# Hybrid block: input normalised before its hi/lo split, gates evicted by ScalarE, ten columns a turn

## What is computed

```python
h = rmsnorm(x, norm_g); proj = h @ w_in
v, bg, cg, za, u, zb, ga, gb = split(proj)      # u, zb: 1024 wide; the others 2048
ya = (bg * causal_conv3(cg * v, conv_w) * silu(za)) @ w_out_a
yb = gelu(s5_scan(u, ...))                       # 64 groups of 64 complex states
yb = yb * sigmoid(yb @ w_glu + b_glu)
yb = (yb * silu(zb)) @ w_out_b
m = sigmoid(ga) * ya + sigmoid(gb) * yb
x = rmsnorm(x + m @ w_o, final_g)
```

## Time and profile before

| | |
|---|---|
| median of 3 runs | 2556.7 us (2553.48 to 2559.24) |
| span of the profiled execution | 2557.4 us; no time of its own is given beside its span |
| TensorE busy | 2394.3 us, 94% of the span, 20536 matmuls |
| VectorE busy | 1687.3 us, 66% |
| ScalarE busy | 967.6 us, 38% |
| GpSimd busy | 331.2 us, 13%, nearly all of it before 626 us |
| DMA | 388.57 MB, mean 152 GB/s |
| mean granted TensorE clock | 0.946 |

### The profile page before, as it was taken

How to read it: one execution, slowest core, us unless ns; L and a number is a source line. 1 busy time by engine, 2 the same in 40 slices (tenths; PEclk the granted TensorE clock), 3 DMA queues, 4 the chain that set the end, 5 groups by cost and what they waited for, 6 DMA issues and landing times.

```text
span 2557.4 us, 52642 instructions
## 1 busy us (share of the span) xinstructions
PE 2394.3 (94%) x20536; PEld 2292.1 (90%) x20536; DVE 1687.3 (66%) x2202; ACT 967.6 (38%) x1164; POOL 331.2 (13%) x200
## 2 busy tenths in 40 slices
PE   7988888889999999789998799899999999999997
PEld 7988888888999999789997577669999999999997
DVE  8688888887555598856698644457656656654444
ACT  4433333333544434343443312234443434433442
POOL 0255555554000000200001100000000000000000
PEclk9999999999999999999998677889999999999999
DMA  6543334433555555345554000015555555556554
GB/s 222 190 141 138 139 139 139 139 138 133 197 191 186 181 172 197 131 156 187 188 169 154 20 2 2 18 60 187 183 188 188 181 188 187 182 170 189 188 181 135
DMA packets 107132, 388.57 MB, mean 152 GB/s; under 512 B 11952, under 2 KB 12080, under 8 KB 106800
## 3 DMA queue, kind: packets, MB, share of 16 engines
q1 hardware_dynamic: 103968, 374.39, 43.2%
q0 software_dynamic: 2080, 8.91, 1.0%
q10 hardware_dynamic: 1008, 4.17, 0.4%
HBM read 385.32 MB, written 2.10 MB: 151 GB/s over the span
## 4 chain that ended last, share of the span: by engine, by line
PE 75%; DVE 13%; issue 7%; POOL 3%; ACT 1%; DVEq 0%; DMA 0%; POOLq 0%; ACTq 0%
PE ps_main L1420 22%; PE ps_main L1421 22%; PE ps_main L1422 22%; DVE w_lo L774 3%; POOL turns L380 2%; PE ps_main L1607 1%; PE ps_aux L1607 1%; PE ps_main L1730 1%; PE ps_main L1731 1%; POOL h_state L384 1%; PE ps_aux L1697 1%; PE ps_aux L1696 1%; DVE f_val L940 1%; DVE m L901 1%; PE ps_main L1613 1%
## 5 line engine op out<-in xcount | busy, mean ns | idle before, releaser
L774 DVE TENSOR_TENSOR w_lo<-w_raw,w_hi 128x1024 fp32r<-128x1024 f32 x718 | 935.1, 1315 | 491.2 <-ACT w_hi L460 477.3
L460 ACT ACTIVATE w_hi<-w_raw 128x1024 fp32r<-128x1024 f32 x718 | 747.0, 1046 | 823.3 <-PE ps_main L1422 814.9
L1420 PE MATMUL ps_main<-xh,w_hi 128*128 128x256 f32 x1792 | 524.4, 293 | 45.3 <-DVE w_lo L774 33.5
L1421 PE MATMUL ps_main<-xl,w_hi 128*128 128x256 f32 x1792 | 513.8, 287 | 0.0
L1422 PE MATMUL ps_main<-xh,w_lo 128*128 128x256 f32 x1792 | 512.6, 286 | 0.0
L1420 PEld LDWEIGHTS ps_main<-xh,w_hi 128*128 128x128 f32 x1792 | 350.4, 196 | 60.6 <-DVE w_lo L774 37.0
L1420 PE MATMUL ps_main<-x3h,w_hi 128*128 128x256 f32 x1408 | 394.4, 280 | 0.0
L1421 PE MATMUL ps_main<-x3l,w_hi 128*128 128x256 f32 x1408 | 392.8, 279 | 0.0
L1422 PE MATMUL ps_main<-x3h,w_lo 128*128 128x256 f32 x1408 | 392.8, 279 | 0.0
L1421 PEld LDWEIGHTS ps_main<-xl,w_hi 128*128 128x128 f32 x1792 | 350.5, 196 | 0.5
L1422 PEld LDWEIGHTS ps_main<-xh,w_lo 128*128 128x128 f32 x1792 | 349.8, 195 | 0.0
(11 more groups left out here) (369 smaller groups left out, 3926.8 us busy)
## 6 DMA issues: line engine op xcount, KB each, us to landing
w_raw<-wmain SPq DMA_DIRECT2D x622, 512.0 KB, 3.3
w_raw<-wdown SPq DMA_DIRECT2D x80, 512.0 KB, 3.6
b_stage<-bst POOLq DMA_DIRECT2D x8, 512.0 KB, 5.4
w_raw<-wdown SPq DMA_DIRECT2D x16, 256.0 KB, 2.7
bias<-bias POOLq DMA_DIRECT2D x8, 384.0 KB, 3.3
x_res<-xt ACTq DMA_DIRECT2D x4, 512.0 KB, 10.8
out<-x_res SPq DMA_DIRECT2D x4, 512.0 KB, 2.6
c_raw<-cs ACTq DMA_DIRECT2D x1, 1024.0 KB, 16.7
```

Of the source, the lines that this page charges most:

```text
L460: nc.scalar.activation(whi[:, s, 0:width], raw[:, s, 0:width], ACT.Copy).then_inc(hi_ready, 1)
L774: V.tensor_tensor(wlo[:, s, 0:width], raw[:, s, 0:width], whi[:, s, 0:width].bitcast(F32), ALU.subtract)\
L1420: nc.tensor.matmul(out, whi[:, s, w], xh_[:, k, :], start=(first and kk == 0), stop=False)
L1421: nc.tensor.matmul(out, whi[:, s, w], xl_[:, k, :], start=False, stop=False)
```

## The change

- The input comes first: x is loaded through two queues, ahead of the weights; ScalarE squares it, VectorE adds in pieces, TensorE sums over the partitions, GpSimd multiplies x by norm_g, VectorE by `rstd`, ScalarE rounds and VectorE takes the rest, in five pieces (`PIECES`), which the first column's matmuls follow. No result needs `rstd` any more. As u and silu(zb) now lie where x lay, x is loaded again during `outb`.
- Gates, u and v are read from PSUM by ScalarE (`drain`); the ways through `tz` and the multiplications by `rstd` go.
- ga moves into the turns: ten columns (za, v, cg, bg, ga, twice), ga in a bank of `aux`, copied out by ScalarE, its sigmoid taken later in `gb`. `gaa` becomes `outa`, 16 columns. The scan's steps get new places.
- c_prime goes to GpSimd. The gelu result is split during `outa`, its rounding on ScalarE; so is the rounding of f in `outb`.
- hi and lo of a tensor are one tensor; counts are renumbered.

```diff
-STREAM = [("u", 8, 2), ("zb", 8, 2), ("conv", 64, 2), ("gb", 16, 2), ("gaa", 32, 2), ("glu", 8, 1),
+STREAM = [("u", 8, 16), ("zb", 8, 16), ("conv", 64, 160), ("gb", 16, 32), ("outa", 16, 32), ("glu", 8, 8),
...
-        SCAN_BU, SCAN_IN, SCAN_Y = (0, 0, 3, 3), (0, 1, 3, 4), (3, 4, 6, 7)
+        SCAN_BU, SCAN_IN, SCAN_Y = (0, 0, 3, 3), (0, 1, 4, 5), (4, 5, 8, 9)
+        KINDS = ("za", "v", "cg", "bg", "ga") * 2
+        PIECES = ((0, 2), (2, 4), (4, 8), (8, 12), (12, 16))
...
         def _(sp):
+            for c in (0, 2):
+                sp.dma_start(x[:, 4 * c:4 * c + 4, :], x_dram[:, 4 * c:4 * c + 4, :]).then_inc(x_loaded[c], 16)
             for s in range(RING):
                 sp.dma_start(raw[:, s, :], wmain[s]).then_inc(w_loaded[s], 16)
+            sp.dma_start(const[:, :], const_dram).then_inc(const_loaded, 16)
...
+            for k in range(4):
+                pool.wait_ge(xsq_ready, k + 1)
+                nc.gpsimd.tensor_tensor(x[:, 4 * k:4 * k + 4, :], x[:, 4 * k:4 * k + 4, :],
+                                        par[:, c + 4 * k:c + 4 * k + 4].unsqueeze(2).to_broadcast([P, 4, L]),
+                                        ALU.mult).then_inc(xg_ready, 1)
...
+            pool.wait_ge(yo_ready, SB)
+            for c in range(4):
+                pool.dma_start(x[:, 4 * c:4 * c + 4, :], x_dram[:, 4 * c:4 * c + 4, :]).then_inc(x_again, 16)
...
+            def conv(i, i0, last=False):
+                for p, kind in enumerate(KINDS):
+                    split_hi(n + 3)
+                    split_hi(n + 4)
+                    if p == 9 and not last:
+                        trig(i + 1)
+                    if kind == "za":
+                        finished(n + 1)
+                        act.wait_ge(ya_ready, At(2 * i0 + q + 1, 2, i).v())
+                        drain(ACT.Silu, gt[:, q, :], bank(g), g)
+                    elif kind == "v":
+                        finished(n + 1)
+                        drain(ACT.Copy, vbuf, bank(g), g)
+                    elif kind == "ga":
+                        finished(n + 1)
+                        nc.scalar.activation(slot(sga, j) ..., aux[:, 3, 0:L], ACT.Copy).then_inc(ga_copied, 1)
...
             n0 = UNIT0["outb"]
-            with act.Fori(0, 4) as i:
-                for b in range(4):
-                    split_hi(At(n0 + b + 3, 4, i))
+            for b in range(16):
+                split_hi(At(n0 + b + 3))
+                act.wait_ge(f_ready, b + 1)
+                nc.scalar.activation(mh[:, b, :], f[:, b % 2, :], ACT.Copy).then_inc(mh_ready, 1)
...
+            for c in range(4):
+                dve.wait_ge(xsq_ready, c + 1)
+                link(V.tensor_tensor(f[:, :, :], sqx[:, 4 * c:4 * c + 2, :], sqx[:, 4 * c + 2:4 * c + 4, :], ALU.add))
...
+            ins.then_inc(acc_ready, 1)
+            split_lo(At(0))
+            dve.wait_ge(root_ready, 1)
+            V.reciprocal(rstd[:, :], tmp[:, 0, :]).then_inc(rstd_ready, 1)
...
+            normal(0)
+            normal(1)
+            split_lo(At(1))
+            for k in range(len(PIECES)):
+                if k + 2 < len(PIECES):
+                    normal(k + 2)
+                normal_lo(k)
+                if k == 2:
+                    split_lo(At(2))
...
+                for p, kind in enumerate(KINDS):
+                    lead(n)
+                    if kind == "cg":
+                        finished(n + 1)
+                        evac(V.tensor_tensor(convc[:, 2:L + 2], bank(g), vbuf, ALU.mult), g)
...
+                    elif kind == "bg":
+                        finished(n + 1)
                         evac(V.tensor_tensor(convv, bank(g), tmp[:, 0, :], ALU.mult), g)
-                        link(V.tensor_tensor(convv, convv, rstd[:, :], ALU.mult))
+                        link(V.tensor_tensor(f[:, 0, :], convv, gt[:, q, :], ALU.mult))
...
+            for b in range(16):
+                split_lo(At(n0 + b + 3))
+                dve.wait_ge(unit_used, n0 + b + 1)
+                evac(V.tensor_tensor(tmp[:, 0, :], bank(g), sgb[:, b, :], ALU.mult), g)
+                V.tensor_tensor(f[:, b % 2, :], tmp[:, 0, :], sga[:, b, :], ALU.add).then_inc(f_ready, 1)
+                if b:
+                    mixed_lo(b - 1)
```

More of the change, by code:

```diff
@@ L510, in _ @@
                 split_hi(At(n0 + 2 * b + 4))
-                gate(ACT.Silu, szb[:, b, :], At(b), At(BLOCK0["zb"] + b))
+                finished(At(n0 + 2 * b + 1))
+                drain(ACT.Silu, szb[:, b, :], bank(At(g0 + b)), At(g0 + b))
             def trig(i):
@@ L1406, in _, with unit @@
                 pe.sem_inc(counted, GO)
-            def unit(n, g, xh_, xl_, kb0, kbs, first, last, split=None):
+            def unit(n, out, xs_, kb0, kbs, first, last, split=None):
                 s = n.c % RING
                 pe.wait_ge(lo_ready, n.v(1))
-                out = main[:, g.c % 4, 0:L]
                 for kk in range(kbs):
@@ L1419, in unit, with bank @@
                         pe.wait_ge(split[0], split[1] + k // (split[2:] or (1,))[0] + 1)
-                    nc.tensor.matmul(out, whi[:, s, w], xh_[:, k, :], start=(first and kk == 0), stop=False)
-                    nc.tensor.matmul(out, whi[:, s, w], xl_[:, k, :], start=False, stop=False)
-                    ins = nc.tensor.matmul(out, wlo[:, s, w], xh_[:, k, :], start=False, stop=(last and kk == kbs - 1))
+                    nc.tensor.matmul(out, whi[:, s, w], xs_[:, 0, k, :], start=(first and kk == 0), stop=False)
+                    nc.tensor.matmul(out, whi[:, s, w], xs_[:, 1, k, :], start=False, stop=False)
+                    ins = nc.tensor.matmul(out, wlo[:, s, w], xs_[:, 0, k, :], start=False, stop=(last and kk == kbs - 1))
                 ins.then_inc(unit_used, 1)
+            def bank(g):
+                return main[:, g.c % 4, 0:L]
             def free(g):
@@ L1483, in _ @@
                 for b in range(4):
-                    column(At(n0 + 2 * b, 8, i), At(g0 + b, 4, i), xh, xl)
-            n0, g0 = UNIT0["gaa"], BLOCK0["gaa"]
-            pe.wait_ge(ya_ready, KB)
-            with pe.Fori(0, 8) as i:
+                    column(At(n0 + 2 * b, 8, i), At(g0 + b, 4, i), xs)
+            n0, g0 = UNIT0["outa"], BLOCK0["outa"]
+            pe.wait_ge(ya_ready, KB + 2)
+            with pe.Fori(0, 4) as i:
                 for b in range(4):
-                    column(At(n0 + 2 * b, 8, i), At(g0 + b, 4, i), *((xh, xl) if b % 2 == 0 else (yah, yal)))
+                    column(At(n0 + 2 * b, 8, i), At(g0 + b, 4, i), yas)
             n0, g0 = UNIT0["glu"], BLOCK0["glu"]
@@ L1492, in _ @@
                 free(At(g0 + b))
[L1493 removed]
+                unit(At(n0 + b), bank(At(g0 + b)), ybs, 0, 8, True, True, (yb_ready, 0, 2) if b == 0 else None)
             n0, g0 = UNIT0["outb"], BLOCK0["outb"]
@@ L1533, in qkv_part @@
                     for b in range(4):
-                        column(At(n0 + 8 * first + 2 * b, 8, i), At(g0 + 4 * first + b, 4, i), nh, nl)
+                        column(At(n0 + 8 * first + 2 * b, 8, i), At(g0 + 4 * first + b, 4, i), ns)
             def over_heads(src):
@@ L1818, in _stream @@
     for j in range(16):
-        for start in (za, v, cg, bg):
+        for start in (za, v, cg, bg, ga):
             out += _units(w_in, blk(start, j))
```

405 lines of the change are left out of this document (221 added, 184 removed).

## The result

The changed kernel takes 2495.4 us (median of four runs, 2490.1 to 2501.3); the kernel before, beside it on the same chip, 2558.0 (2553.5 to 2562.0). The ratio is 0.9757 (95% interval 0.9736 to 0.9777): faster by 2.4%, about 62 us. The forecast was 2498 us and a gain of 58.

The account below looks back on a forecast made before the run. TensorE bounds most stages, but full turns lose 11.9 us to waits and half clock. Terms -90.0 + 23.6 + 6 - 4 + 6 = -58.4 take the span from 2557.4 to 2499, time 2498 us (own range 2487 to 2520).

Parts of the forecast that it names:

- The first gate: Stage `gaa`: its 64 units become 32, so 16 columns at 5.63 us leave a stretch without slack, -90.0 us.
- The turns: Eight turns with 20 units instead of 16: seven of 67.0 us and a last of 64.1, +23.6 us.
- unit 15's wait: In each full turn: TensorE wants unit 15 at 48.2, its split is ready at 50.1, a 2.0 us stall.
- the clock's 0.7: In each full turn: a clock fall costing 2.3 us, taken in one turn of three, 0.7 us.
- No stall: Turns: the ring's lead absorbs unit 15's lateness, turns of 64.1 us, time 2478 us; chance 0.18.
- One old stall stays: Turns: VectorE still 4.8 us behind during the angles, 3.4 lost to the clock, turn 72.3, time 2535; chance 0.16.
- The turn keeps its loss: Turns: GpSimd's hold on VectorE is the real bound, each keeps its 11.9 us, turn 76.0, time 2567; chance 0.04.
- The fourth: Start and `outb` both at their bounds, turns as forecast: 2507 us; included in the forecast's chance of 0.60.
- The start: Before the first columns: all of x must arrive and be normalised first, third column near 41 us, +6 us.
- `glu`: Before `glu`: the scan output's eight roundings no longer stand alone but beside the `outa` columns, -4 us.
- `outb`: Stage `outb`: lag grows 0.7 us a unit, about seven units are free, some eight pay, +6 us.
- The ring of 3.54 us: In `outb`: each unit's closed way through hand-over, copy, conversion, split and eviction takes 3.54 us against 2.81.

Follow-up runs that it names:

- the run with the gate apart: Changed kernel with the first gate's 16 columns in their own stage behind the turns, old turn positions restored: 2547.0 us, ratio 0.9951 to the kernel before.
- the reordered kernel: Changed kernel with VectorE doing unit 15's split ahead of the turn's fourth scan input: 2489.7 us, ratio 0.9736 to the kernel before.
- the two runs above: Changed kernel with weights held until x's first quarter landed: 2498.6 us; changed kernel with VectorE, not GpSimd, scaling by norm_g at the start: 2497.7 us.

## Why the prediction was right

**The first gate (-90.0 forecast, -90.7).** 16 columns of 5.63 us out of a stretch without slack: right, and the run with the gate apart put a number on the other half of the argument, 5.0 us a turn for 11.3 us of work.

**The turns (+23.6 forecast, +19.9).** The layout by hand found the one wait, its unit and its cause, and the absence of the wait for the scan state. Its terms were each off by less than a microsecond, and in both directions: the turn's work is 64.7 us (the last turn, and the turns of the reordered kernel), not 64.1; unit 15's wait costs 1.7 (the row's 1.44 and the restart), not 2.0, and unit 13's 0.2 did not come; and the clock's 0.7 was not paid once. 64.7 + 1.7 = 66.4 against 67.0. (The lower bound of +4 for the eight turns should read +3.3, 8 x 64.1 less 509.5; nothing hangs on it.)

**The rivals.** "No stall" (2478) missed by 2.3 us a turn, the wait's 1.7 and the 0.6 by which the turn's work is longer; as a kernel with another order it exists, and its turns are 64.7. "One old stall stays" needed unit 11 to be late, and it was not. "The turn keeps its loss" is refuted most plainly by the window of 466 matmuls. The fourth, start and `outb` both at their bounds, came half true: 9.7 of 10 and 7.7 of 11, and the turns paid less.

**The start (+6 forecast, +9.7).** The mechanism was right, two sizes were not. I let x land near 8.5, from a rate of 364 GB/s; the same window now shows 233, and the last quarter was squared from 12.9. And I allowed "about one addition" to each of the four scalings, of 1.8 us; there were four held ones, at 2.00 to 2.27, and the scalings themselves took 2.2 to 2.3: the sum was ready at 21.2, not at 17, past the 19 that I had called the worst. That is the term that was mis-sized, by 4 us at TensorE's first weights: by the two runs above, the matmuls start 3.9 earlier without the held additions and 1.1 earlier with the earlier landing. That the sum came out right all the same is in part luck: the start's 3.7 us above its term and the turns' 3.7 below cancel.

**`glu` (-4 forecast, -3.8) and `outb` (+6 forecast, +7.7).** The ring of 3.54 us measured 3.46. The lag met TensorE only after twelve of the 16 units, where seven were forecast, so `outb` itself paid 2.8 us (48.1 against 45.3), not 6. But the lag went on into `wo`, where it cost 5.0: a wait of 0.46 us, one of 2.19 for the last `ml`, and some 2.3 at half clock. The sum had left that out, so that 7.7 against 6 is nearer than its parts.

**The clock.** The granted clock stayed at 1.00 in all turns of the changed kernel (waits of 1.44 us) and of the one with drains on VectorE (0.80 and 1.99). It fell to the lower level at the wait of 2.88 us in all seven full turns of the kernel with the gate apart, at its second wait (1.9 to 2.6) in three of the seven, at the 2.19 in `wo`, and at the 4.79 before the change. The prediction took one fall in three turns, and leaned for it on the earlier trace rows, a wait of 2.64 us with full clock behind it; that row is the exception among the eight turns of that trace. In the other seven the matmuls behind that wait run at half clock, as here behind the 2.47 at 363.57:

```profile
364.93 0.58 PE L1420 MATMUL ps_main<-xh,w_hi 128*128 128x256 f32 x1
```

So one fall in three turns was too low a price for waits of that length (2.3 to 2.6 us); it did no harm, since the wait that came was 1.44. The Trainium skill, "TensorE: Matmul & The Clock Gate", section "HAM oscillation", warns that a wait in each step of a loop can pay the clock's fall every time; the waits of its example are longer than these. The kernel before and the one with the gate apart agree with it, turn for turn. Had it come true here, the seven turns would have cost some 11 us more than forecast (an estimate, at 2.3 us a fall); with waits of 1.44 us the traces show no fall.

## What to carry to other kernels

Work in a full stage of its own costs its whole length; inside a loop in which its engine waits for others it costs only what the wait doesn't cover (here 40 us for 90). Before moving instructions, write the order of the late engine in one turn beside what the bound engine wants next: a wait that ends on a split can be a matter of one instruction's place, and here an edit of five lines (9.0 us) was worth half of what the drains were (17.7). And keep instructions on GpSimd short where VectorE has work due on SBUF: here its instructions of 0.42 to 0.69 us lasted 2.0 to 2.3 beside GpSimd's of about 2.2, and 8.73 beside one of 8.87.

## What the runs showed that I had not expected

- The attention stage has two lengths in the same program, 41.4 to 43.3 or 48.5 to 50.1 us, with a granted clock of 0.87 or 0.51 near its end in the two profiles shown. One profile of each kernel can differ by 8 us there with no cause in the code.
- An instruction of 0.43 us on VectorE stood for 8.73 us beside one long one of GpSimd, in both kernels, and TensorE idled 16.8 us behind it. In 16 pieces GpSimd's pass took 16.1 us instead of 8.9, and the program still gained 10.
- A scaling of a quarter of x took GpSimd 2.2 to 2.3 us beside VectorE's additions, where a quarter of the long one is 1.8 (7.08 for four). Whether that is VectorE's doing or a cost of each shorter instruction, no run separates.
- Late in `outb` TensorE's waits were only 0.36 us a unit; the one of 2.19 that followed in `wo` brought a stretch at half clock.
